# Stick-breaking attention weights written in place over their logarithms, on one Trainium2 core

## The chip, the cores and the metric

The kernel is one program on one core of a Trainium2 chip. It computes two small models one after the other from inputs in the chip's memory. The metric is the device time of one execution in microseconds (us). The engines are TensorE (PE in the rows; PEld its weight loads), VectorE (DVE), ScalarE (ACT), GpSimd (POOL) and SyncE (SP), which issues the loads of the weights.

## The reference

The first block (two layers: differential attention and mLSTM, then a gated spatial mixer) comes first and is not touched. The second block begins with a hybrid mixer over 16 meta tokens and 512 tokens of width 1024. Cut to what matters, its attention is:

```python
def stick_breaking_attention(q, k, v):          # (B, L, 16 heads, 64)
    for q0, q1 in bounds:                       # the 16 meta tokens, then blocks of 128 queries
        z = einsum("bqhd,bkhd->bhqk", q[:, q0:q1], k[:, :q1]) * scale
        log_beta = log_sigmoid(z)
        log_fail = where(causal, log_beta - z, 0.0)
        survive = cumsum(log_fail, axis=3, reverse=True) - log_fail
        a = where(causal, exp(log_beta + survive), 0.0)
        o = einsum("bhqk,bkhd->bqhd", a, v[:, :q1])
```

Beside it run a short causal convolution with gates, two projections with sigmoid gates, an output projection, and after the mixer a gated MLP.

## The kernel before

Every matmul is in float32 and is made of three passes over a weight that is rounded into a high part and a rest: ScalarE writes `w_hi` from `raw` (`split`, L652), VectorE writes `w_lo` (its `split`, L2119), and TensorE multiplies hi by hi, hi by lo and lo by hi. SyncE loads a weight tile of 128 x 1024 into one of four slots of `raw`. ScalarE and VectorE make a tile ready three tiles ahead (`AHEAD`) of its use.

The input projection of the second block goes in eight pairs of heads (`p` = 0 to 7). A pair takes eight weight tiles (`t` = 0 to 7): q, k, v, b, c, h and the two gates. A tile is made in two halves of the tokens (`halves`, L1799 to L1801), each of 24 matmuls into its own bank of `pj`, and the next tile writes the same two banks. So each bank must be emptied within the time of one half. `take` on ScalarE copies q (L1056), k (L1058), v, b (L1068) and c (L1070) out of it, VectorE's L2776 (`conv_in`) multiplies c with the sixth tile, h, for the convolution and so empties tile 5's banks, and ScalarE's tanh (L1073) empties those of tiles 6 and 7.

The attention of pair p-1 is threaded through pair p. It has four query blocks, d = 0 to 3, with (d+1) x 128 keys and the 16 meta keys, for two heads at once. After the even tile t = 2d TensorE does `pair_scores` (scores of block d into `zz`, counted in the semaphore `z`) and then `turn_pair` of block d-1, counted in `turned`; after tile 0 those are block 0 and block 3 of the pair before that. A `turn_pair` transposes the weights of 16 meta keys from `s_am`, and 2(d+1) squares of 128 x 128 from `s_a` into `tr`. At the head of the odd tile t = 2d+1 ScalarE does `logs` of block d: Abs of `zz` into `s_e` (L1035, or L1037 and L1038 for d = 3), Exp (L1039) and Ln (L1040) in place; behind that on its queue stand a `split` and the copies of that tile. VectorE waits for the logarithms and does `weights` (L2679): maximum and sum (L2691), two scans (L2697), and a difference (L2702), all in `s_e`; in tile 5 the second `conv_in` stands between the scans and the difference. In the next even tile ScalarE's own `weights` takes the exponential of `s_e` into `s_am` (L1046) and `s_a` (L1047), counted in `a`. VectorE's `copy_turned` (L2709, L2710) waits for `turned` and copies the transposed weights out of `tr` and `aux`, and `pair_values` multiplies them with v.

The attention of pair 7 is threaded in the same way through the eight tiles of the projection of the convolution (`branch`), after `c_hi` and `c_lo` have been made of the convolution's output; there VectorE's gate products L2721 empty `pj`. After it, `items` (L1992 to L1996) multiply the attention's output `a_hi`, and wait for all the gate products.

The order of each engine's work is written out by hand; an engine does its instructions in order and waits on counting semaphores.

Of the kernel before, what the change touches and what calls it, by code (L numbers as in the profile page):

```python
# [17 lines left out]
ACT = mybir.ActivationFunctionType  # L18
# [5 lines left out]
P = 128  # L24
# [15 lines left out]
def need(eng, sem, n):  # L40

    if not (isinstance(n, int) and n <= 0):
        eng.wait_ge(sem, n)
# [23 lines left out]
def two_models(  # L67
# [6 lines left out]
    _, T, D = x.shape  # L74
    KD = D // P
    NT = T // P
    NM = meta_tokens_2.shape[0]
# [53 lines left out]
    with ExitStack() as ctx:  # L131
# [3 lines left out]
        def sems(stage, names):  # L135
            return {n: sem(f"{stage}_{n}") for n in names.split()}
# [9 lines left out]
        def sb(reg, name, shape, dt=F32):  # L146
            n = 2 if dt == BF16 else 4
            for s in shape[1:]:
                n *= s
            t = nc.alloc_sbuf_tensor_at(name, shape, dt, offset=reg[1])  # L150
            reg[1] += (n + 31) // 32 * 32
            assert reg[1] <= reg[2] + 31, (name, reg)
            return t

        def again(reg, skip=0):
            return [reg[0], reg[0] + skip, reg[2]]

        const = region(4960 + 4 * P + 64 + 4 * NM)
        ident = sb(const, "ident", [P, P])
# [105 lines left out]
        w_ = again(W)  # L265
# [15 lines left out]
        w_ = again(W)  # L281
# [21 lines left out]
        w_ = again(W, 218272 - 187488)  # L303
# [17 lines left out]
        w_ = again(W)  # L321
# [26 lines left out]
        w_ = again(W)  # L348
# [10 lines left out]
        w_ = again(W, AT_W)  # L359
# [1 line left out]
        cc, cv = turns(("cc", [P, TA]), ("cv", [P, TA]))  # L361
        cx = sb(w_, "cx", [P, TA + KW2 - 1])
        s_e = sb(w_, "s_e", [P, 2, TF])
        s_a = sb(w_, "s_a", [P, 2, T])
        s_zm = sb(w_, "s_zm", [P, 2, NM])
        s_am = sb(w_, "s_am", [P, 2, NM])
        s_aT = sb(w_, "s_aT", [P, 2, NT, P])
# [5 lines left out]
        w_ = again(W)  # L373
# [14 lines left out]
        def bank(name, n=1):  # L388
            return ctx.enter_context(nc.psum_tensor(name, [P, n, 512], F32))
# [3 lines left out]
        tr = bank("tr", 2)  # L393
# [28 lines left out]
        MX = sems("mix", "half q k v b c x g conv vturned vtok z log w a turned probsT pv o ychi yclo pc "  # L422
                         "meta_step ahi alo pa mhi mlo")
# [220 lines left out]
        def _(act):  # L644
# [61 lines left out]
            for name, src in ROWS[0]:  # L706
                a = col[name][1]
# [137 lines left out]
            for c in range(NT):  # L845
                ins = act.activation(m_kd0[:, 1, c, :], zz[:, 0, c * P:(c + 1) * P], ACT.Exp, bias=acol[:, c, 0:1])
# [180 lines left out]
            def logs(pr, d, table=True):  # L1027

                n, j = (d + 1) * P, pr * NT + d
                if table and d in (0, NT - 1):  # L1030
                    act.preload_act_table_set("natural_log_exp_and_others")
                act.wait_ge(MX["z"], j + 1)
                need(act, MX["a"], j)
                if d < NT - 1:
                    link(act.activation(s_e[:, :, 0:NM + n], zz[:, :, 0:NM + n], ACT.Abs))  # L1035
                else:
                    act.activation(s_e[:, :, NM:NM + n], zz[:, :, 0:n], ACT.Abs)  # L1037
                    link(act.activation(s_e[:, :, 0:NM], s_zm[:], ACT.Abs))  # L1038
                link(act.activation(s_e[:, :, 0:NM + n], s_e[:, :, 0:NM + n], ACT.Exp, scale=-1.0))  # L1039
                act.activation(s_e[:, :, 0:NM + n], s_e[:, :, 0:NM + n], ACT.Ln, bias=1.0).then_inc(MX["log"], 1)  # L1040

            def weights(pr, d):
                n, j = (d + 1) * P, pr * NT + d
                act.wait_ge(MX["w"], j + 1)
                need(act, MX["turned"], j)
                act.activation(s_am[:], s_e[:, :, 0:NM], ACT.Exp)  # L1046
                act.activation(s_a[:, :, 0:n], s_e[:, :, NM:NM + n], ACT.Exp).then_inc(MX["a"], 1)  # L1047

            def take(t, p, par, hf, first, src=None):

# [45 lines left out]
            def pair(p, par, prev=True, prev2=True, first=False):  # L1096

                for t in range(8):
                    if first and t < NSLOT:
                        if t == 0:  # L1100
                            first_four()
                        continue
                    if t % 2 and prev:
                        logs(p - 1, t // 2)
                    split(P_0 + t + AHEAD, p, 8)
                    if t < 5:
                        act.wait_ge(MX["half"], p * 8 + (t + 1))
                        take(t, p, par, 0, not prev2)
                    if t == 0 and prev2:
                        weights(p - 2, NT - 1)  # L1110
                    if t and t % 2 == 0 and prev:
                        weights(p - 1, t // 2 - 1)
                    if t > 5:
                        act.wait_ge(MX["half"], p * 8 + (t + 1))
                        take(t, p, par, 0, not prev2)
                    if t != 5:
                        finished(P_0 + t, p, 8)
                        take(t, p, par, 1, not prev2)
# [32 lines left out]
            branch(0)  # L1151
            meta_logs()
            weights(p - 1, NT - 1)
            branch(1)
            act.wait_ge(MX["meta_step"], META_STEP["weights"])
            act.activation(s_me[:], s_me[:], ACT.Exp).then_inc(MX["meta_step"], 1)
            logs(p, 0, table=False)
            branch(2)
            weights(p, 0)
            logs(p, 1)  # L1160
            branch(3)
            branch(4)
# [104 lines left out]
        def _(pe):  # L1267
# [131 lines left out]
            for r, n in enumerate(nrows):  # L1399
                ins = pe.transpose(tt[:, 0, r * P:r * P + n], vrow[0:n, r, :], ident[0:n, 0:n])  # L1400
            ins.then_inc(S["turned"], 1)
            pe.wait_ge(S["meta_in"], 32)
            for k in range(KD):
                ins = pe.transpose(rb[:, 0, (KD + k) * NM:(KD + k + 1) * NM], mt[:, k * P:(k + 1) * P],
                                   ident[0:NM, 0:NM])
            pe.wait_ge(S["meta_step"], SETUP_META["scaled"])
            for k in range(KD):
                ins = pe.transpose(rb[:, 0, k * NM:(k + 1) * NM], xmeta[:, k * P:(k + 1) * P], ident[0:NM, 0:NM])
# [174 lines left out]
            for c in range(NT):  # L1583
                ins = pe.matmul(zz[:, 0, c * P:(c + 1) * P], ident_b[:], mask_ge[:], start=False, stop=(c == NT - 1),
                                skip_group_check=True)
# [6 lines left out]
            for c in range(NT):  # L1592
                ch = slice(c * P, (c + 1) * P)
                ins = pe.matmul(zz[:, 1, ch], m_kT[:, ch], m_qT[:, ch], start=True, stop=True)
            ins.then_inc(ML["products"], 1)
            pe.wait_ge(DA["y"], HD - 1)
            for t in range(NT):
                ins = pe.transpose(rb[:, 0, t * P:(t + 1) * P], m_kT[:, t * P:(t + 1) * P], ident[:])
# [143 lines left out]
            for g in range(SG):  # L1742
                ins = pe.transpose(zz[:, g // NT, (g % NT) * P:(g % NT + 1) * P], wsp[:, g, :], ident[:])
            ins.then_inc(SV["turned"], 1)
            for b, dst in enumerate((oo, aux)):
                ins = pe.matmul(dst[:, 0, :], ones[0:1, :], brow[:, b * NT:(b + 1) * NT, :], start=True, stop=True)
# [79 lines left out]
            def turn_pair(pr, d):  # L1826
                j = pr * NT + d
                pe.wait_ge(MX["a"], j + 1)
                need(pe, MX["probsT"], j)
                pe.transpose(aux[0:2 * NM, 0, 512 - P:512], s_am[:].rearrange("p c n -> p (c n)"), ident[:])  # L1830
                for c in range(2):
                    for k in range(d + 1):
                        ins = pe.transpose(tr[:, c, k * P:(k + 1) * P], s_a[:, c, k * P:(k + 1) * P], ident[:])  # L1833
                ins.then_inc(MX["turned"], 1)

            def pair_values(pr, d, par):
# [1232 lines left out]
```

## Time and profile before

| | us |
|---|---|
| median of 3 runs | 1941.81 |
| lowest and highest | 1941.48, 1943.69 |
| the profiled execution, its own time | 1941.62 |
| its span in the trace | 1939.9 |
| TensorE busy | 1924.9 |
| VectorE, ScalarE, GpSimd busy | 1030.8, 764.8, 67.0 |
| mean granted clock of TensorE | 0.999 of full |

The span is the time between the first and the last instruction that the profiler records. A matmul's record is longer than the step from one matmul to the next, since they are pipelined: in the second block's projection a matmul starts every 0.12 us and is recorded with 0.28. So TensorE's busy time says only that it hardly ever stood idle. In the timeline a row gives the start, the duration, and in brackets the idle time before it on its engine and what ended that. `x2` at a row's end merges two instructions. The second block's projection lies between about 985 and 1388 us of the span, the projection of the convolution between 1389 and 1452.

### The profile page before, as it was taken

Reading aid. Unit: us, or ns where it says so; the run is one execution under the profiler, and the core shown is the slowest. Engines: PE = TensorE matmul, PEld = TensorE weight load, DVE = VectorE, ACT = ScalarE, POOL = GpSimd, SP = SyncE. Lnnn points to the kernel's source line nnn. Section 1 sums busy time; section 2 is a strip of 40 time slices with the busy share of each in tenths; the row PEclk is TensorE's granted clock in tenths of the full one; section 3 lists DMA queues with packets and bytes.
Section 4 is the critical chain, followed back from the end, with each engine's and each line's share of the span. In section 5 each row is a group of like instructions: output and inputs, shape, how many; then the busy total and the mean of one; then the engine's idle time right before and its main releaser. Section 6 shows DMA issues by size and latency. Waiting matters only on the chain.

```text
span 1939.9 us, 31396 instructions
## 1 busy us (share of the span) xinstructions
PE 1924.9 (99%) x12104; PEld 1695.6 (87%) x12104; DVE 1030.8 (53%) x1601; ACT 764.8 (39%) x1268; POOL 67.0 (3%) x118
## 2 busy tenths in 40 slices
PE   8999999999999999999999999999999999999998
PEld 8888888889888788888999999999999798999886
DVE  5777767544253555532645655555766364444333
ACT  5544443333233333322435555555642243323222
POOL 3000000000020000000100000000000010000000
PEclk9999999999999999999999999999999999999999
DMA  6222212232323333323232222222222232333321
GB/s 175 80 68 74 76 55 77 78 85 87 119 77 98 99 88 89 91 89 120 79 96 77 67 76 77 74 80 66 69 74 88 77 109 87 91 94 96 104 92 55
DMA packets 244004, 167.27 MB, mean 86 GB/s; under 512 B 5294, under 2 KB 231702, under 8 KB 243911
## 3 DMA queue, kind: packets, MB, share of 16 engines
q1 hardware_dynamic: 242224, 160.98, 27.9%
q10 hardware_dynamic: 1286, 4.23, 0.7%
q8 instruction: 70, 1.15, 0.2%
q0 software_dynamic: 400, 0.72, 0.1%
q14 instruction: 24, 0.19, 0.0%
HBM read 163.81 MB, written 2.10 MB: 86 GB/s over the span
## 4 chain that ended last, share of the span: by engine, by line
PE 97%; DVE 2%; DMA 1%; ACT 0%; issue 0%; SPq 0%; POOL 0%; ACTq 0%; DVEq 0%
PE pj L1799 9%; PE pj L1801 9%; PE pj L1800 9%; PE pj L1279 8%; PE pj L1280 8%; PE pj L1281 8%; PE zz L1280 2%; PE zz L1279 2%; PE zz L1281 2%; PE zz L1336 2%; PE tr L1336 2%; PE zz L1338 2%; PE tr L1338 2%; PE tr L1337 2%; PE zz L1337 2%; PE pj L1336 2%
## 5 line engine op out<-in xcount | busy, mean ns | idle before, releaser
L2119 DVE TENSOR_TENSOR w_lo<-raw,w_hi 128x1024 fp32r<-128x1024 f32 x299 | 365.1, 1223 | 276.6 <-ACT w_hi L652 273.6
L652 ACT ACTIVATE w_hi<-raw 128x1024 fp32r<-128x1024 f32 x299 | 314.5, 1055 | 214.7 <-PE tr L1338 141.2
L1799 PE MATMUL pj<-x_hi,w_hi 128*128 128x258 f32 (+1 forms) x1280 | 365.0, 285 | 0.0
L1801 PE MATMUL pj<-x_hi,w_lo 128*128 128x258 f32 (+1 forms) x1280 | 361.6, 283 | 0.0
L1800 PE MATMUL pj<-x_lo,w_hi 128*128 128x258 f32 (+1 forms) x1280 | 361.0, 282 | 0.0
L1279 PE MATMUL pj<-x_hi,w_hi 128*128 128x512 f32 x632 | 254.0, 402 | 0.0
L1280 PE MATMUL pj<-x_lo,w_hi 128*128 128x512 f32 x632 | 249.8, 395 | 0.0
L1281 PE MATMUL pj<-x_hi,w_lo 128*128 128x512 f32 x632 | 248.4, 393 | 0.0
L1800 PEld LDWEIGHTS pj<-x_lo,w_hi 128*128 128x128 f32 x1280 | 241.7, 189 | 0.8
L1799 PEld LDWEIGHTS pj<-x_hi,w_hi 128*128 128x128 f32 x1280 | 241.3, 189 | 0.9
L1801 PEld LDWEIGHTS pj<-x_hi,w_lo 128*128 128x128 f32 x1280 | 241.3, 189 | 0.0
L1281 PEld LDWEIGHTS pj<-x_hi,w_lo 128*128 128x128 f32 x632 | 118.9, 188 | 27.0
L1279 PEld LDWEIGHTS pj<-x_hi,w_hi 128*128 128x128 f32 x632 | 118.8, 188 | 26.7 <-issue 0.8
L1280 PEld LDWEIGHTS pj<-x_lo,w_hi 128*128 128x128 f32 x632 | 118.8, 188 | 25.2
L1542 PE MATMUL pj<-w_hi,x_hi 128*128 128x256 f32 x256 | 72.8, 285 | 0.0
L1543 PE MATMUL pj<-w_hi,x_lo 128*128 128x256 f32 x256 | 71.9, 281 | 0.0
L1544 PE MATMUL pj<-w_lo,x_hi 128*128 128x256 f32 x256 | 71.9, 281 | 0.0
L2709 DVE COPY s_aTm<-oa 32x128 f32<-32x128 f32 x32 | 8.9, 278 | 110.2 <-PE tr L1833 110.1
L1280 PE MATMUL zz<-x_lo,w_hi 128*128 128x512 f32 x160 | 63.5, 397 | 0.0
L1279 PE MATMUL zz<-x_hi,w_hi 128*128 128x512 f32 x160 | 63.0, 394 | 0.0
L1281 PE MATMUL zz<-x_hi,w_lo 128*128 128x512 f32 x160 | 62.9, 393 | 0.0
L586 POOL TENSOR_SCALAR n_ms<-n_ms 128x1 f32<-128x1 f32 x32 | 14.2, 445 | 1339.0 <-ACT scaled L671 1302.8
(601 smaller groups left out, 3712.3 us busy)
## 6 DMA issues: line engine op xcount, KB each, us to landing
raw<-in_l_w_in_dram SPq DMA_DIRECT2D x113, 512.0 KB, 4.1
raw<-in_w_in_dram SPq DMA_DIRECT2D x64, 512.0 KB, 4.0
raw<-in_w_up_gate_dram SPq DMA_DIRECT2D x44, 512.0 KB, 3.8
raw<-in_l_w_out_dram SPq DMA_DIRECT2D x32, 512.0 KB, 3.4
raw<-in_w_down_dram SPq DMA_DIRECT2D x22, 512.0 KB, 3.4
raw<-in_w_proj_conv_dram SPq DMA_DIRECT2D x8, 512.0 KB, 4.0
raw<-in_w_proj_attn_dram SPq DMA_DIRECT2D x8, 512.0 KB, 4.1
raw<-in_w_out_dram SPq DMA_DIRECT2D x8, 512.0 KB, 3.5
```

The lines of the kernel that those rows point to most:

```text
L652: act.activation(w_hi[:, slot], raw[:, slot], ACT.Copy).then_inc(hi_done, 1)
L1279: pe.matmul(dst, w_hi[:, slot, k, :], hi(k), start=(first and k == 0), stop=False)
L1280: pe.matmul(dst, w_hi[:, slot, k, :], lo(k), start=False, stop=False)
L1281: ins = pe.matmul(dst, w_lo[:, slot, k, :], hi(k), start=False, stop=(last and k == KD - 1))
L1336: pe.matmul(dst[:, nh, :], hi[:, k, tok], w_hi[:, slot, w, :], start=start, stop=False)
L1337: pe.matmul(dst[:, nh, :], lo[:, k, tok], w_hi[:, slot, w, :], start=False, stop=False)
L1338: ins = pe.matmul(dst[:, nh, :], hi[:, k, tok], w_lo[:, slot, w, :], start=False, stop=stop)
L1542: pe.matmul(dst, x_hi[:, k, tok], wh, start=(k == 0), stop=False)
L1799: pe.matmul(dst, w_hi[:, slot, k, :], hi[:, k, tok], start=(k == 0), stop=False)
L1800: pe.matmul(dst, w_hi[:, slot, k, :], lo[:, k, tok], start=False, stop=False)
L1801: ins = pe.matmul(dst, w_lo[:, slot, k, :], hi[:, k, tok], start=False, stop=(k == KD - 1))
L2119: dve.tensor_tensor(w_lo[:, slot], raw[:, slot], w_hi[:, slot].bitcast(F32), ALU.subtract).then_inc(lo_done, 1)
```

## The change

The weights are no longer written into a buffer of their own. ScalarE's `weights` writes the exponential over the logarithms in `s_e`, past the 16 meta columns, and `turn_pair` transposes from there. `s_a` is gone, and the buffers behind it move up in memory. Since `logs` of the next block overwrites `s_e`, it now waits until the turns of the block before are done (`turned`) in place of the exponentials (`a`). `weights` no longer waits for `turned`, which the wait in `logs` covers.

```diff
@@ buffers
-        s_a = sb(w_, "s_a", [P, 2, T])
@@ ScalarE, logs
                 act.wait_ge(MX["z"], j + 1)
-                need(act, MX["a"], j)
+                need(act, MX["turned"], j)
@@ ScalarE, weights
                 act.wait_ge(MX["w"], j + 1)
-                need(act, MX["turned"], j)
                 act.activation(s_am[:], s_e[:, :, 0:NM], ACT.Exp)
-                act.activation(s_a[:, :, 0:n], s_e[:, :, NM:NM + n], ACT.Exp).then_inc(MX["a"], 1)
+                act.activation(s_e[:, :, NM:NM + n], s_e[:, :, NM:NM + n], ACT.Exp).then_inc(MX["a"], 1)
@@ TensorE, turn_pair
-                        ins = pe.transpose(tr[:, c, k * P:(k + 1) * P], s_a[:, c, k * P:(k + 1) * P], ident[:])
+                        ins = pe.transpose(tr[:, c, k * P:(k + 1) * P], s_e[:, c, NM + k * P:NM + (k + 1) * P], ident[:])
```

The waits as they stand in the instructions: ScalarE's queue in tiles 5 and 6 of a pair in the loop over pairs, before. The semaphores of this stage have `mix_` before their names.

```order
L1032 REGISTER_ALU
L1035 ACTIVATE s_e<-zz 128x2x400 [waits mix_a,mix_z]
L55 REGISTER_ALU
L1039 ACTIVATE s_e<-s_e 128x2x400 [waits act_chain]
L55 REGISTER_ALU
L1040 ACTIVATE s_e<-s_e 128x2x400 [waits act_chain]
L652 ACTIVATE w_hi<-raw 128x1024 [waits tile_done,raw_in0]
L651 REGISTER_ALU [waits raw_in1]
L652 ACTIVATE w_hi<-raw 128x1024 [waits tile_done]
L1046 ACTIVATE s_am<-s_e 128x32 [waits mix_turned,mix_w]
L1047 ACTIVATE s_a<-s_e 128x2x384
L1114 REGISTER_ALU
```

And the same stretch with the change:

```order
L1031 REGISTER_ALU
L1034 ACTIVATE s_e<-zz 128x2x400 [waits mix_turned,mix_z]
L55 REGISTER_ALU
L1038 ACTIVATE s_e<-s_e 128x2x400 [waits act_chain]
L55 REGISTER_ALU
L1039 ACTIVATE s_e<-s_e 128x2x400 [waits act_chain]
L651 ACTIVATE w_hi<-raw 128x1024 [waits tile_done,raw_in0]
L650 REGISTER_ALU [waits raw_in1]
L651 ACTIVATE w_hi<-raw 128x1024 [waits tile_done]
L1044 ACTIVATE s_am<-s_e 128x32 [waits mix_w]
L1045 ACTIVATE s_e<-s_e 128x2x384
L1112 REGISTER_ALU
```

The instructions and their order stay; the Abs at the head waits for `turned` where it waited for `a`, the Exp of the meta columns waits for the difference alone, and the Exp of the keys, the row below it, writes `s_e`.

ScalarE's queue in tile 7, before (`REGISTER_ALU` and `ISA` rows are the queue's own waits and counters):

```order
L1037 ACTIVATE s_e<-zz 128x2x512 [waits mix_a,mix_z]
L1038 ACTIVATE s_e<-s_zm 128x2x16
L55 REGISTER_ALU
L1039 ACTIVATE s_e<-s_e 128x1056 [waits act_chain]
L55 REGISTER_ALU
L1040 ACTIVATE s_e<-s_e 128x1056 [waits act_chain]
L652 ACTIVATE w_hi<-raw 128x1024 [waits tile_done,raw_in2]
L1114 REGISTER_ALU
L1073 ISA [waits mix_half]
L1073 ACT_TABLE_LOAD
L1073 ACTIVATE gates<-pj,hbg 128x258
L656 REGISTER_ALU
```

With the change:

```order
L1036 ACTIVATE s_e<-zz 128x2x512 [waits mix_turned,mix_z]
L1037 ACTIVATE s_e<-s_zm 128x2x16
L55 REGISTER_ALU
L1038 ACTIVATE s_e<-s_e 128x1056 [waits act_chain]
L55 REGISTER_ALU
L1039 ACTIVATE s_e<-s_e 128x1056 [waits act_chain]
L651 ACTIVATE w_hi<-raw 128x1024 [waits tile_done,raw_in2]
L1112 REGISTER_ALU
L1071 ISA [waits mix_half]
L1071 ACT_TABLE_LOAD
L1071 ACTIVATE gates<-pj,hbg 128x258
L655 REGISTER_ALU
```

Between the Abs with its new wait and the tanh of `gates` the queue is as it was.

## Rows read from the trace of the kernel before

**Rows 1.** The page's part 1, and the list of waits (us in total, times, longest).

```profile
PE 1924.9 (99%) x12104; PEld 1695.6 (87%) x12104; DVE 1030.8 (53%) x1601; ACT 764.8 (39%) x1268; POOL 67.0 (3%) x118
PE pj L1799 <- DVE gates L2721: 0.5, 1, 0.5
```

**Rows 2.** Timeline, tile 5 of two pairs: start us, us, engine, line, operation [idle before <-releaser].

```profile
1196.01 0.84 ACT L1035 ACTIVATE s_e<-zz 128x800 f32<-128x800 f32 x1 [1.42 <-PE zz L1822]
1196.55 0.28 DVE L2709 COPY s_aTm<-oa 32x128 f32<-32x128 f32 x1 [5.51 <-PE tr L1833]
...
1199.64 1.23 DVE L2119 TENSOR_TENSOR w_lo<-raw,w_hi 128x1024 fp32r<-128x1024 f32 x1 [2.21 <-ACT w_hi L652]
...
1204.31 0.43 DVE L2776 TENSOR_TENSOR cx<-cc,pj 128x258 f32<-128x258 f32 x1 [0.21 <-DVE s_e L2697]
1204.97 0.28 PE L1799 MATMUL pj<-x_hi,w_hi 128*128 128x258 f32 x1
...
1375.35 0.42 DVE L2776 TENSOR_TENSOR cx<-cc,pj 128x258 f32<-128x258 f32 x1
...
1376.17 0.28 PE L1799 MATMUL pj<-x_hi,w_hi 128*128 128x258 f32 x1
```

**Rows 3.** Timeline, ScalarE, TensorE and VectorE around tile 7 of the same pair.

```profile
1208.81 1.28 ACT L1031 ACT_TABLE_LOAD   x1
...
1210.12 1.03 ACT L1037 ACTIVATE s_e<-zz 128x1024 f32<-128x1024 f32 x1
...
1210.89 0.28 DVE L2709 COPY s_aTm<-oa 32x128 f32<-32x128 f32 x1 [1.08 <-PE tr L1833]
...
1215.77 0.48 ACT L1073 ACTIVATE gates<-pj,hbg 128x258 f32 x1
...
1216.42 0.34 PE L1799 MATMUL pj<-x_hi,w_hi 128*128 128x258 f32 x1
...
1216.72 0.48 ACT L1073 ACTIVATE gates<-pj,hbg 128x258 f32 x1 [0.47 <-PE pj L1801]
```

**Rows 4.** Timeline, the heads of tiles 1 and 3 of the next pair.

```profile
1224.10 0.41 ACT L1035 ACTIVATE s_e<-zz 128x288 f32<-128x288 f32 x1
...
1225.07 0.28 DVE L2709 COPY s_aTm<-oa 32x128 f32<-32x128 f32 x1 [3.18 <-PE tr L1833]
...
1228.00 0.39 ACT L1058 ACTIVATE s_k<-pj 128x264 f32<-128x264 f32 x1 [1.58 <-PE pj L1801]
...
1238.89 0.63 ACT L1035 ACTIVATE s_e<-zz 128x544 f32<-128x544 f32 x1 [1.73 <-PE zz L1822]
...
1239.21 0.28 DVE L2709 COPY s_aTm<-oa 32x128 f32<-32x128 f32 x1 [5.54 <-PE tr L1833]
```

**Rows 5.** Timeline, TensorE waits for a gate product in the conv projection.

```profile
1396.32 0.76 DVE L2721 SCALAR_TENSOR_TENSOR gates<-gates,pj 128x258 f32<-128x258 f32 x2
...
1396.89 0.35 PE L1799 MATMUL pj<-c_hi,w_hi 128*128 128x258 f32 x1 [0.55 <-DVE gates L2721]
1397.09 0.28 PE L1800 MATMUL pj<-c_lo,w_hi 128*128 128x258 f32 x1
```

**Rows 6.** Timeline, the last pair's attention in the conv projection.

```profile
1439.30 0.41 DVE L2721 SCALAR_TENSOR_TENSOR gates<-gates,pj 128x258 f32<-128x258 f32 x1
...
1440.30 0.28 PE L1799 MATMUL pj<-c_hi,w_hi 128*128 128x258 f32 x1
...
1444.66 1.03 ACT L1037 ACTIVATE s_e<-zz 128x1024 f32<-128x1024 f32 x1 [3.75 <-PE zz L1822]
...
1451.85 0.42 DVE L2721 SCALAR_TENSOR_TENSOR gates<-gates,pj 128x258 f32<-128x258 f32 x1
...
1452.33 0.39 PE L1992 MATMUL pj<-a_hi,w_hi 128*128 128x258 f32 x1
```

**Rows 7.** Busy time by stretch: PE, PEld, DVE, ACT, POOL (count); granted clock, DMA share, GB/s.

```profile
1395.00:1400.00 5.00, 4.46 (x50) 4.23 (x48) 4.93 (x23) 2.86 (x6) 0.00 (x0) 1.00 0.00 0
...
1421.00:1426.00 5.00, 5.00 (x31) 4.72 (x30) 1.12 (x1) 2.21 (x4) 0.00 (x0) 0.66 0.37 105
```

## The prediction

> **What bounds the kernel now.** I read the page first. TensorE is busy for 1924.9 us, 99% of the span, and in the list of waits it stood, in the whole execution, waiting for VectorE on the second block's `pj` for 0.5 us in all, once [rows 1]. So nothing the change does to ScalarE's or VectorE's busy time matters; what matters is whether it makes TensorE wait. For that I read the timeline of one pair tile by tile. A pair is eight weight tiles (0 to 7), each of two halves of 24 matmuls, 2.87 us a half at 0.12 us a matmul. After an even tile TensorE does the attention work: the scores of block d into `zz`, then the turns of block d-1. ScalarE meets the new scores at the head of the next odd tile, and behind `logs` on its queue stand the rounding of a weight tile and the copies that empty `pj`.
>
> **What the change does to that queue.** Arithmetic and counts stay: 32 exponentials write `s_e` where they wrote `s_a`, and 160 transposes read it. In place costs nothing that a row shows: L1039 and L1040 already work from `s_e` to `s_e`. One wait moves. `weights` no longer waits for `turned`; that wait was long satisfied (the turns of block d-1 end a whole tile earlier), so it gives nothing. `logs` waits for `turned` instead of `a`. TensorE issues the turns right behind the scores, so ScalarE's Abs, which now starts 0.04 us after the last score matmul, will start after the last transpose. VectorE's copy L2709 waits for just that semaphore today, so its start is my measure of the release. The Abs moves by the difference of the two rows: for d=2, 1196.55 - 1196.01 = 0.54 us [rows 2]; for d=3, 1210.89 - 1210.12 = 0.77 us [rows 3]; for d=0 of the next pair, 1225.07 - 1224.10 = 0.97 us, and for d=1, 1239.21 - 1238.89 = 0.32 us [rows 4]. Everything queued behind the Abs on ScalarE moves along, unless it had idle time before it.
>
> **Tile 1 and tile 3 (d=0, d=1): nothing.** In tile 1 the first copy behind, `s_k`, had 1.58 us of idle before it [rows 4]; 0.97 fits. In tile 3 everything may slip by the 0.32; the copy `cb` behind it empties a half bank that TensorE wants again only after one more half, 2.87 us. VectorE's w_lo slips too, but a tile is rounded three tiles (some 17 us) ahead of its use. If that cover were gone, each pair would cost up to 1.3 us more.
>
> **Tile 5 (d=2): seven times.** Abs, Exp, Ln and then the rounding end 0.54 later, and VectorE's w_lo sits idle waiting for exactly that rounding (2.21 us idle, released by w_hi) [rows 2]. Behind it on VectorE, back to back, stand the first conv product, the block's maximum and scans, and the second conv product, L2776, which frees the second half of `pj` for tile 6. It ends at 1204.74 and TensorE starts that half at 1204.97 [rows 2]: 0.23 us. What a release costs I take from the one existing stall of this kind: VectorE's first gate product starts at 1396.32 and, at 0.42 us (the row of one such product in [rows 6]), ends at 1396.74; TensorE starts at 1396.89, so 0.15, and the matmul behind comes after 0.20 instead of 0.12 us, another 0.08 for a restart [rows 5]. Slack is therefore 0.23 - 0.15 = 0.08, and the stall 0.54 - 0.08 + 0.08 = 0.54 us. Four pairs look like this. In the first and the last two, which stand outside VectorE's loop, L2776 ends 0.40 before its reader (1375.77 against 1376.17) [rows 2]: 0.54 - 0.25 + 0.08 = 0.37 us. Sum: 4 x 0.54 + 3 x 0.37 = **3.3 us**. Bounds: 0 (if a release takes no longer and VectorE picks the delay up in its idle 2.21) and 7 x 0.62 = 4.3.
>
> **Tile 7 (d=3): seven times, the last one mild.** Abs, Abs of `s_zm`, Exp, Ln, rounding, a table load of 1.28 us and the gate's tanh run on ScalarE without a gap from 1210.12 to 1216.25, 6.13 us. The tanh empties the first half of `pj`, and TensorE starts the next pair's tile 0 there at 1216.42, 0.17 us later [rows 3]. That is what a release costs (0.15 above), and the distance is the same 0.17 at all six places where a pair follows a pair: TensorE starts on the release, and the slack is zero. The 0.77 us passes in full, with 0.08 for the restart: 0.85 x 6 = 5.1. (A stall in tile 6 shifts scores, turns and ScalarE alike, so the two do not cover each other.) After the seventh pair comes the first tile of the conv projection, whose bank waits through c_hi and c_lo. These stand behind the second gate, which has 0.47 us of idle before it in every pair [rows 3], so that 0.77 - 0.47 = 0.3 is left at most; the second gate also starts a little before the first has ended, and I take 0.2. Together **5.3 us**; bounds 0 and 7 x 0.85 = 6.0.
>
> **The last pair's attention, inside the projection.** The weight tiles here have more attention work between them. For d=2 the gate product behind the logarithms ends at 1439.71, 0.59 us before its reader at 1440.30 [rows 6]: 0.54 - 0.59 + 0.15 = 0.1, with the restart 0.2; d=0 and 1 have more room. Tight is d=3: Abs 1444.66 and the same 0.77 to the end of the turns, through rounding, w_lo and the block's maximum to the gate product that ends at 1452.27; TensorE starts the output of `a_hi` at 1452.33, waiting for it [rows 6]: 0.8. Together **1.0 us**, bounds 0 and 1.1. VectorE's scan and weights shift with it, TensorE too, so the last turn costs nothing more.
>
> **Sum.** 3.3 + 5.3 + 1.0 = 9.6 us. The profiled execution took 1941.6 us (1.7 around its span), 0.2 under the median shown, so 1951.2 and, against the median, 1951.4; I say 1951.3.
>
> **A rule against this change.** The rows show ScalarE 0.77 us ahead of the turns, which the second buffer allows it, and TensorE with hardly a gap [rows 1, 3]. The Trainium skill, in "Perfetto Trace Analysis", section "Optimization Strategy", says that a gap that repeats on the engine that should be saturated can mean too few buffers in SBUF. By that rule every one of the 31 hand-overs of the one buffer left would show as a gap, and the sum would be the second rival's 19.8 us in place of 9.6.
>
> **Rivals.**
> *Only the hard deadline costs.* Tile 5's delay vanishes in VectorE's idle time or in a shorter release. For: 2.21 us of idle stand there. Against: that idle is waiting for the very rounding that is late. 1941.8 + 5.3 + 0.8 = 1947.9. 7%.
> *Every block pays.* If no idle time and no bank time covers anything, each Abs's lateness comes out at the end: 8 x (0.32 + 0.54 + 0.77) + 7 x 0.97 = 19.8 us: 1961.6. Against: 1.58 us idle in tile 1. 3%.
> *The clock.* After the small matmuls of the meta queries the granted clock averages 0.66 in 1421 to 1426, and is 1.00 (2.4 GHz) in 1395 to 1400 [rows 7]: for part of these 5 us it was at 1.2 GHz, and 0.34 x 5 = 1.7 us were lost. All else stays as forecast, but this work now comes 8.5 us later. If the drop does not come: 1949.6, 30%. If the new stalls bring more of them (each 1.7, two to four), 1954.5 to 1958, 5%; against that, the existing stall of 0.55 us lies in a clock of 1.00 [rows 5, 7]. The Trainium skill, "TensorE: Matmul & The Clock Gate", Part 1, has the clock follow how busy the engine has lately been; no run here yet shows whether 0.85 us pauses count.
> *Not slower.* One mechanism: ScalarE is released not by the last transpose but reaches the Abs later anyway. In tile 7 a table load ends at 1210.09 [rows 3]; if it came 0.8 us later, the turns would be done and the new wait would be free, in tile 7 and by the same lateness in tile 5, where there is no table load. Then nothing is left of 9.6, and the clock's 1.7 may come back: 1940 to 1942. It decides from 1210.89, the release; ScalarE is 0.77 us ahead of it in every pair. That the change does not do what it says belongs here, if the release of `turned` had come first all along; the rows show Abs ahead of L2709 each time. 3%.
>
> **How the numbers follow.** Forecast with its exact mechanism 52%, and 30% for the same with the clock back; 7, 3, 5 and 3% for the rest. A measurement of this kernel tells about 0.2% (3.9 us) from no change, so slower means over 1945.7: all but the last rival and a little of the first, 0.95; same 0.04, faster 0.01. The range leaves out the outer rivals: low 1948.4 (the clock back and no restart cost, 1949.6 less 15 x 0.08), high 1953.2 (all stalls at their upper bounds, 11.4).
>
> **What would show it.** In the new profile: Abs of d=2 and d=3 start with L2709, and their idle is laid to the transposes. TensorE's waits gain a row on the gates' tanh (six, about 0.8 each) and one on L2776 (seven, 0.3 to 0.5). Tiles 1 and 3 keep their pace. TensorE's busy time stays near 1925 us while the span grows by 9 to 10. ScalarE's `weights` starts no earlier against TensorE. I am wrong if the stalls are there but the span is not longer by their sum, or if tile 0 starts within 0.1 us of its old distance from tile 7.

## The result, and the profile after

| | before | with the change |
|---|---|---|
| median, us | 1941.77 (5 runs) | 1952.71 (5 runs) |
| all, us | 1941.48, 1941.75, 1941.77, 1941.81, 1943.69 | 1950.94, 1951.25, 1952.71, 1952.90, 1952.91 |
| ratio, 95% interval | | 1.0049, 1.0037 to 1.0060 |
| the profiled execution | 1941.62 | 1952.91 |

The kernel before ran again beside each group of experiments, and their ratios are against these runs: median 1941.96 us (26 runs) for `wait_only`, `two_buffers`, `own_d3` and `own_d2`, 1943.14 (16 runs) for `own_d2_w3`, `turns_first` and the two with a doubled Abs, 1942.91 (22 runs) for `scores_first`, `turns_first_sa` and `spread_meta`; one of these last 22 was a slow execution of 4422.14 us, which the ratios leave out.

The changed kernel is slower by 0.5%. The page of its profile, parts 1 and 4, against [rows 1] and against part 4 of the page before (second fence): TensorE's busy time grew by 5 us and the span by 11.3, and the chain of work that ended last now passes through ScalarE and VectorE for 3% each, where it was 0% and 2%.

```profile
span 1951.2 us, 31365 instructions
PE 1930.1 (99%) x12104; PEld 1697.5 (87%) x12104; DVE 1030.5 (53%) x1601; ACT 762.3 (39%) x1268; POOL 66.8 (3%) x118
PE 92%; DVE 3%; ACT 3%; issue 2%; DMA 1%; SPq 0%; ACTq 0%; POOL 0%; DVEq 0%
```

```profile
PE 97%; DVE 2%; DMA 1%; ACT 0%; issue 0%; SPq 0%; POOL 0%; ACTq 0%; DVEq 0%
```

TensorE's list of waits (us in total, times, longest) has three rows that were not there, six waits for the gates' tanh, four for the second conv product, and one for the last gate product. The wait for `c_lo`, at the head of the conv projection, was there before with 0.4 us (second fence, from the trace before) and has grown to 0.6:

```profile
PE pj L1797 <- ACT gates L1071: 3.7, 6, 0.6
PE pj L1797 <- DVE cx L2774: 1.1, 4, 0.3
PE pj L1990 <- DVE gates L2719: 0.9, 1, 0.9
PE pj L1310 <- DVE c_lo L2806: 0.6, 1, 0.6
```

```profile
PE pj L1312 <- DVE c_lo L2808: 0.4, 1, 0.4
```

These waits are shorter than the stalls, since a matmul is recorded with 0.28 us and the next is due 0.12 us after its start: idle appears only past the recorded end. So I read a stall from the distance between the starts. In the timeline of the changed kernel, tile 5 of the pair that [rows 2] show:

```profile
1200.77 0.28 DVE L2707 COPY s_aTm<-oa 32x128 f32<-32x128 f32 x1 [5.23 <-PE tr L1831]
1200.83 0.84 ACT L1034 ACTIVATE s_e<-zz 128x800 f32<-128x800 f32 x1 [2.03 <-PE tr L1831]
...
1204.46 1.23 DVE L2117 TENSOR_TENSOR w_lo<-raw,w_hi 128x1024 fp32r<-128x1024 f32 x1 [2.81 <-ACT w_hi L651]
...
1209.13 0.42 DVE L2774 TENSOR_TENSOR cx<-cc,pj 128x258 f32<-128x258 f32 x1 [0.21 <-DVE s_e L2695]
...
1209.61 0.39 PE L1797 MATMUL pj<-x_hi,w_hi 128*128 128x258 f32 x1 [0.27 <-DVE cx L2774]
```

The Abs starts 0.06 us behind the copy that waits for the turns, and its idle time is laid to the transposes. VectorE's idle before w_lo grew from 2.21 to 2.81 us, and TensorE stands waiting for the conv product. Tile 7 and the head of the next pair, against [rows 3, 4]:

```profile
1215.70 1.03 ACT L1036 ACTIVATE s_e<-zz 128x1024 f32<-128x1024 f32 x1 [0.79 <-PE tr L1831]
...
1221.34 0.84 ACT L1071 ACTIVATE gates<-pj,hbg 128x258 f32 x2
1221.96 0.36 PE L1797 MATMUL pj<-x_hi,w_hi 128*128 128x258 f32 x1 [0.63 <-ACT gates L1071]
...
1230.71 0.41 ACT L1034 ACTIVATE s_e<-zz 128x288 f32<-128x288 f32 x1 [1.05 <-PE tr L1831]
...
1233.58 0.39 ACT L1056 ACTIVATE s_k<-pj 128x264 f32<-128x264 f32 x1 [0.56 <-PE pj L1799]
```

The tanh of the first half starts at 1221.34, ends 0.48 later (its duration in [rows 3]) at 1221.82, and TensorE starts at 1221.96. In tile 1 the idle before `s_k` shrank from 1.58 to 0.56 us, and TensorE noticed nothing.

Of the growth of 11.3 us, 9.6 are there when TensorE starts L1990, at 1461.97 where it was 1452.33 [rows 6]. Not all of that is the change: TensorE is 0.36 us later already behind the first scores, before any block meets the new wait (the second matmul behind them starts at 998.35 where it was 997.99), and 0.28 of that is there after the first 10 us of the program. In the traces of the other versions that place lies between 0.15 us early and 0.42 late, once the clock is allowed for, so this is spread between executions, and 9.3 us belong to the change. The other 1.7 come at a place that the change does not touch. Busy time by stretch (PE, PEld, DVE, ACT, POOL; granted clock, DMA share, GB/s) and the timeline there:

```profile
1425.00:1435.00 10.00, 10.00 (x72) 9.29 (x71) 5.92 (x10) 3.90 (x7) 0.00 (x0) 0.83 0.38 105
1555.00:1560.00 5.00, 5.00 (x24) 4.26 (x24) 1.48 (x4) 0.11 (x1) 0.00 (x0) 0.66 0.00 0
```

```profile
1553.89 1.91 PE L2041 MATMUL oa<-sel,hl_t 8*128 8x4 f32 x16 [0.24 <-DVE hl_t L2914]
1555.73 0.67 PE L1334 MATMUL pj<-w_hi,m_hi 128*128 128x512 f32 x1
```

The half-clock stretch of [rows 7] is still there (1425 to 1435 is that work, later), and there is a second one behind 16 small matmuls of 4 columns. The kernel before has the same 16 small matmuls, and in its profiled execution no fall comes behind them:

```profile
1544.19 1.92 PE L2043 MATMUL oa<-sel,hl_t 8*128 8x4 f32 x16 [0.24 <-DVE hl_t L2916]
1546.04 0.50 PE L1336 MATMUL pj<-w_hi,m_hi 128*128 128x512 f32 x1
```

Such a stretch costs 1.7 us and comes or stays away from one execution to the next. That fits the times of each kernel, which stand in groups some 1.3 to 2.0 us apart. The mean granted clock goes with them: in the changed kernel it is 0.999 for the two executions of the lower group and 0.998 for the three of the upper. In what follows I compare profiled executions after taking off 1.7 us for each half-clock stretch: without any, before comes to 1939.9 and the changed kernel to 1949.5, a difference of 9.6. With the spread of 0.4 us at the start, a difference of this kind is good to about half a microsecond.

### The profile page after: what moved, and what is told of

It reads as the page before. It is cut to its first block, busy times and chain, and to the rows that moved or that the text cites. A ratio compares the mean times of both kernels' runs of the same rounds, so it can differ in the third digit from the quotient of the medians.

```text
span 1951.2 us, 31365 instructions
## 1 busy us (share of the span) xinstructions
PE 1930.1 (99%) x12104; PEld 1697.5 (87%) x12104; DVE 1030.5 (53%) x1601; ACT 762.3 (39%) x1268; POOL 66.8 (3%) x118
## 4 chain that ended last, share of the span: by engine, by line
PE 92%; DVE 3%; ACT 3%; issue 2%; DMA 1%; SPq 0%; ACTq 0%; POOL 0%; DVEq 0%
PE pj L1797 8%; PE pj L1799 8%; PE pj L1798 8%; PE pj L1277 8%; PE pj L1278 8%; PE pj L1279 7%; PE zz L1278 2%; PE zz L1277 2%; PE zz L1279 2%; PE zz L1334 2%; PE pj L1334 2%; PE tr L1334 2%; PE zz L1336 2%; PE tr L1336 2%; PE pj L1336 2%; PE tr L1335 2%
```

## The experiments

**1. Is it the wait or the in-place write?** The kernel before with the waits alone:

```diff
-                need(act, MX["a"], j)
+                need(act, MX["turned"], j)
...
                 act.wait_ge(MX["w"], j + 1)
-                need(act, MX["turned"], j)
```

> The kernel before with the waits of the change and nothing else: the weights still go to s_a. My theory (the wait alone costs, by making the logarithms start after the turns): the same time as the changed kernel, before + 9.6 us, some 1951.4, or 1.7 more in executions in which the clock drops once more; TensorE's stalls before tile 0 (six, 0.92 us gap between matmuls) and before tile 6's second half (four of 0.56, three of 0.39) are all there. Rival (writing and turning in place costs, by the buffer or the moved addresses): most of the 9.6 goes away, 1942 to 1945.

Measured: 1951.06 us median (1950.77 to 1952.50), ratio 1.0049 (1.0035 to 1.0063). The profiled execution has one half-clock stretch, 1951.06, so 1949.4 without. Its waits are those of the changed kernel to the tenth:

```profile
PE pj L1798 <- ACT gates L1072: 3.7, 6, 0.6
PE pj L1798 <- DVE cx L2775: 1.1, 4, 0.3
```

The whole loss is the wait, within 0.1 us. Writing in place, and reading the transposes from there, costs nothing that shows.

**2. In place with two buffers.** The changed kernel with `s_e0` (400 columns) for blocks 0 and 2 and `s_e1` for 1 and 3 (the cut leaves out that `weights` waits for `turned` again, since `s_am` is still one buffer, and that each user picks its buffer from the list; the same holds for experiments 3 and 4):

```diff
-        s_e = sb(w_, "s_e", [P, 2, TF])
+        s_e0 = sb(w_, "s_e0", [P, 2, 400])
+        s_e1 = sb(w_, "s_e1", [P, 2, 528])
+        s_es = [s_e0, s_e1, s_e0, s_e1]
...
-                need(act, MX["turned"], j)
+                need(act, MX["turned"], j - 1)
```

> The changed kernel, in place, but with two buffers s_e, one for blocks 0 and 2 (cut to the 400 columns that they need) and one for blocks 1 and 3; the logarithms wait for the turns of two blocks before. My theory: all stalls gone, within 0.5 us of the kernel before, 1941.8. Rival (in place costs): stays at 1950 or more. Rival (the clock): small differences of 1.7 us from it in some executions.

Measured: 1942.94 us median (1941.53 to 1945.01, 11 runs), ratio 1.0004 (0.9995 to 1.0013). The profiled execution took 1941.53 with one stretch, none of the new waits, and the clock fell at the other place (1545 to 1550) and not at the first:

```profile
1415.00:1435.00 20.00, 20.00 (x168) 18.98 (x166) 12.77 (x22) 9.20 (x15) 0.00 (x0) 1.00 0.20 57
1545.00:1550.00 5.00, 5.00 (x22) 4.25 (x21) 1.23 (x4) 1.09 (x2) 0.00 (x0) 0.66 0.00 0
```

**3. A buffer of its own for block 3.** `s_es = [s_e0, s_e0, s_e0, s_e1]`, and the wait in `logs`:

```diff
-                need(act, MX["turned"], j)
+                need(act, MX["turned"], (j - 1, j, j, j - 3)[d])
```

> The changed kernel with a buffer of its own for block 3 alone, so the wait is free for block 3 (tile 7) and stays for block 1 and 2. My theory: tile 7's 5.3 and the 0.8 at the end go, tile 5's 3.3 and 0.2 stay: before + 3.5, 1945.3. Rival (only the hard deadline of tile 7 costs, and the rest comes from the clock or elsewhere): 1941.8 to 1943. Rival (each block pays its lateness, 19.8 us cut down by something): tile 3's 8 x 0.32 would stay as well, + 6.

Measured: 1946.81 us median (1945.45 to 1948.91, 10 runs), ratio 1.0024 (1.0014 to 1.0033). The profiled one took 1946.67 with two stretches, 1943.3 without: 3.4 above before, for 3.5 expected. The wait of block 0 is relaxed here too, for the block before it in the buffer is now block 2; tile 1 had room in any case. TensorE's waits keep the conv product and lose the gates' tanh:

```profile
PE pj L1800 <- DVE cx L2777: 1.1, 4, 0.3
```

**4. A buffer of its own for block 2.** `s_es = [s_e0, s_e0, s_e1, s_e0]`, with the waits `(j, j, j - 3, j - 1)[d]`.

> The changed kernel with a buffer of its own for block 2 alone, so the wait is free in tile 5 and stays in tiles 1, 3 and 7. My theory: tile 5's 3.5 goes and 6.1 stay: 1947.9, with TensorE's six gaps of 0.92 us before tile 0 and none above 0.13 before tile 6's second half. The savings of this and of the own buffer for block 3 add up to the whole loss, since a stall shifts scores, turns and ScalarE alike. Rival (the two stalls cover each other): each alone saves less than its part, the two savings sum to under 8.

Measured: 1943.41 us median (1940.29 to 1945.25, 11 runs), ratio 1.0004 (0.9995 to 1.0013), so 4.5 us less than I expected. The fault lay in the experiment. With block 2 elsewhere, block 3 overwrites what block 1 left, whose turns are done before tile 5 begins, so its wait in tile 7 had come free as well. Two blocks of four still share a buffer with their forerunner here (0 and 1), and nothing is lost: a small confirmation that tiles 1 and 3 have room. (For block 0 the forerunner is block 3 of the pair before.) The second try keeps block 3's wait, `(j, j, j - 3, j)[d]`.

> The kernel with a buffer of its own for block 2, once more, now with the wait of the change kept for block 3: in the run before, block 3's last user of the buffer was block 1, so its wait had come free as well and nothing of tile 7's cost was left in it. My theory: tile 5's stalls are gone, tile 7's six (0.92 us gap before tile 0) and the last pair's stay: before + 6.1, so 1947.9 with as many clock drops as the kernel before has in most executions, 1949.6 with one more. Rival (tile 7's deadline bites only when tile 5 has been late): under 1945.

Measured: 1948.41 us median (1947.95 to 1949.85, 6 runs), ratio 1.0030 (1.0018 to 1.0043). The profiled one took 1949.79 with two stretches, 1946.4 without: 6.5 above before, for 6.1 expected. One wait of the six was longer here (0.9 against some 0.6 for the rest), and that is most of the excess.

```profile
PE pj L1800 <- ACT gates L1074: 4.1, 6, 0.9
```

Its two stretches, with the columns as above:

```profile
660.00:670.00 10.00, 10.00 (x34) 7.08 (x33) 5.66 (x9) 1.84 (x3) 1.03 (x1) 0.83 0.57 168
1550.00:1560.00 10.00, 9.76 (x49) 8.19 (x48) 3.78 (x9) 1.97 (x5) 2.07 (x4) 0.83 0.01 2
```

Here a third place had the half clock, in the first block, behind four matmuls whose operands have a single row (`brow` and `ones`, 1.98 us for the four). 3.4 and 6.5 make 9.9, where the whole is 9.6 (with the start of each execution taken into account 3.6 and 6.4, and 9.3): the two stalls do not cover each other.

**5. The lateness without the wait.** The kernel before, with both buffers and its own waits, and the Abs of block 3 done twice:

```diff
+                    link(act.activation(s_e[:, :, NM:NM + n], zz[:, :, 0:n], ACT.Abs))
                     act.activation(s_e[:, :, NM:NM + n], zz[:, :, 0:n], ACT.Abs)
...
```

(The other changed line gives ScalarE's loop its new count of chained instructions.)

> The kernel before with the Abs of block 3 done twice, one after the other (1.03 us more on ScalarE at the head of tile 7, no wait added and no buffer taken away). My theory (zero slack from ScalarE's Abs in tile 7 to the next pair's tile 0): TensorE's gap before tile 0 grows from 0.17 to about 1.2 six times, 6 x 1.13 = 6.8, 0.5 behind the seventh pair, 1.1 at the end: before + 8.4, 1950.2. Rival (it is the wait for another engine, and not its lateness, that costs): before + 0 to 2.

Measured: 1951.15 us median (1950.91 to 1952.71, 5 runs), ratio 1.0046 (1.0032 to 1.0060). The profiled one took 1951.24 with two stretches, 1947.8 without: 7.9 above before, for 8.4. So it is ScalarE's lateness that costs, with the new wait or without it:

```profile
PE pj L1800 <- ACT gates L1074: 5.3, 6, 0.9
```

The same for blocks 0 and 1:

```diff
+                if d < 2:
+                    link(act.activation(s_e[:, :, 0:NM + n], zz[:, :, 0:NM + n], ACT.Abs))
...
```

> The kernel before with the Abs of blocks 0 and 1 done twice (0.41 and 0.63 us more at the head of tiles 1 and 3, sixteen times). My theory (tiles 1 and 3 have room): within 0.5 us of the kernel before. Rival (every block pays its lateness): 8 x (0.45 + 0.66) = 8.9 more, 1950.7.

Measured: 1943.14 us median (1941.48 to 1943.65, 11 runs), ratio 1.0002 (0.9993 to 1.0011), and no new wait of TensorE; the profiled one took 1941.48 with one stretch. Sixteen delays of 0.4 to 0.6 us vanish in tiles 1 and 3.

**6. Can one buffer be had for nothing?** TensorE's attention work in another order, in the changed kernel and in the kernel before (abridged, each word stands for the lines of that step):

```diff
                     if t % 2 == 0:
-                        (values) (scores) (turns)
+                        (turns) (scores) (values)
```

> The changed kernel, one buffer, with TensorE's attention work in another order in the pairs: turns, then scores, then the values, where it was values, scores, turns. Scores then end with the turns already done, and as the values (0.68 to 0.90 us) are longer than the turns (0.46 to 0.74), no later than in the kernel before. My theory: all stalls in the pairs gone, the 1.0 us of the last pair stays (its order is not changed): 1942.8. Rival (a single buffer costs by itself, in whatever order): 1950 or more. Rival (the new order only moves the wait, to TensorE's turns waiting for the weights): a new row of PE tr waiting for ScalarE's exponentials, some 1945.

> The kernel before (both buffers, its own waits) with the order turns, scores, values in the pairs. In the changed kernel this order took away all stalls, and yet each of the 32 gaps between two tiles was 0.23 us longer, so 7.4 us. My theory: the order alone costs this on TensorE (the load of 64-row scores behind 128-row transposes), so before + 7.4: 1949.3 with one clock drop, 1951 with two. Rival (the 0.23 comes from reading the transposes from s_e, or from ScalarE at work in the same buffer): within 1 us of before.

Measured with one buffer: 1950.73 us median (1949.10 to 1950.96, 5 runs), ratio 1.0040 (1.0026 to 1.0054); the profiled one 1950.73 with two stretches, 1947.3 without, 7.4 above before where 1.0 was expected. With both buffers: 1949.17 us median (1947.87 to 1950.02, 6 runs), ratio 1.0034 (1.0022 to 1.0046); the profiled one 1948.59 with one stretch, 1946.9 without, 7.0 above before where 7.4 were expected (0.4 of the 7.0 are there before the first pair's attention, so 6.6). My theory for the first run was wrong, and its stalls were gone all the same: TensorE's waits have neither the tanh nor the conv product. The time went into TensorE's own work. The gap after tile 6, before (first fence) and with turns first in one buffer (second):

```profile
1207.72 0.28 PE L1801 MATMUL pj<-x_hi,w_lo 128*128 128x258 f32 x1
1207.84 0.38 PE L1843 MATMUL oa<-s_aTm,s_vmp 128*128 128x128 f32 x2
1208.15 0.66 PE L1847 MATMUL oa<-s_aT,s_vt 128*64 128x128 f32 x8
1208.74 1.13 PE L1815 MATMUL zz<-s_k,s_q 64*128 64x512 f32 x4
1209.80 0.28 PE L1822 MATMUL zz<-mask_lt,ident_b 128*128 128x128 bf16 x2
1209.92 0.27 PE L1830 MATMUL oa<-ident,s_am 128*32 128x128 f32 x1
1210.03 0.82 PE L1833 MATMUL tr<-ident,s_a 128*128 128x128 f32 x6
1210.61 0.37 PE L1799 MATMUL pj<-x_hi,w_hi 128*128 128x258 f32 x1
```

```profile
1210.94 0.28 PE L1799 MATMUL pj<-x_hi,w_lo 128*128 128x258 f32 x1
1211.07 0.27 PE L1828 MATMUL oa<-ident,s_am 128*32 128x128 f32 x1
1211.17 0.82 PE L1831 MATMUL tr<-ident,s_e 128*128 128x128 f32 x6
1211.92 1.13 PE L1813 MATMUL zz<-s_k,s_q 64*128 64x512 f32 x4
1212.98 0.29 PE L1820 MATMUL zz<-mask_lt,ident_b 128*128 128x128 bf16 x2
1213.11 0.44 PE L1841 MATMUL oa<-s_aTm,s_vmp 128*128 128x128 f32 x2
1213.47 0.66 PE L1845 MATMUL oa<-s_aT,s_vt 128*64 128x128 f32 x8
1214.06 0.39 PE L1797 MATMUL pj<-x_hi,w_hi 128*128 128x258 f32 x1
```

From the last projection matmul to the first of the next tile it is 2.89 us before and 3.12 with the other order, for the same instructions. Six transposes take 0.58 us to the start of what follows when that is the projection, and 0.75 when it is the scores, whose weights have 64 rows; the first values take 0.36 instead of 0.31. Not 32 gaps grew, as I had put into the expectation of the second run, but 27, 26 of them by 0.23 and one by 0.06: 6.05 in all. With the 1.0 of the last pair that makes 7.1 of the 7.4 of the first run; and the matmul behind each of the 26 gaps comes 0.02 to 0.03 later than before, while the six waits of 0.05 before tile 0 are gone. That 32 x 0.23 also gives 7.4 was chance: the 1.0 of the last pair was in the time that I had divided. The second run shows that it is the order and not the buffer, since it has the same gaps with `s_a` kept. Why scores behind transposes cost more is not shown: eight values take 0.59 us to what follows them whether that is the scores or the projection.

**7. The scores first.** The kernel before in the order scores, values, turns.

> The kernel before (both buffers, its own waits) with TensorE's attention work in the pairs in the order scores, values, turns. ScalarE meets the scores 0.7 to 0.9 us earlier. My theory: the six waits of 0.05 us before tile 0 go, and the first tile of a pair is paced by TensorE alone: 0.3 us less than before, 1941.5 in executions with one clock drop, which no median can tell apart; the trace's gap before tile 0 goes from 0.17 to 0.12. Rival (what stands beside what on TensorE counts for more, as in the order with turns first, where each of the 32 gaps was 0.23 us longer): before + 1 to 7 us.

Measured: 1946.83 us median (1943.86 to 1948.82, 11 runs), ratio 1.0016 (1.0007 to 1.0025); the profiled one 1945.38 with one stretch, 3.8 above before. The rival held: the gap after tile 6 is 3.05 us, 0.16 longer, and 26 gaps of this kind, 4.2 us, outweigh the 0.3 us won. The order of the kernel before is the shortest of the three.

**8. The clock.** The kernel before, with the eight small value products of the meta queries (16 matmuls in the trace, two for each) laid one by one between the eight steps of a projection tile:

```diff
-            meta_queries(3)
             pair_values(p, 0, 1)
-            branch(4)
...
+            branch(4, between=meta_value)
```

> The kernel before with the eight small value products of the meta queries (4 columns each, 1418.8 to 1420.8 us) laid one by one between the eight steps of the next projection tile, same work. My theory of the clock (a stretch of small matmuls lets the granted clock fall to 1.2 GHz for a few us, 1.7 us lost, at one of three places from execution to execution): the granted clock stays 1.00 from 1415 to 1435 and executions of some 1940.2 and 1941.9 appear in place of 1941.8 and 1943.4. Rival (the drop comes at a fixed time, or from the attention work): the half-clock stretch stays, and the time with it.

Measured: 1946.54 us median (1942.03 to 1947.00, 11 runs), ratio 1.0015 (1.0006 to 1.0024); the profiled one 1945.48 with two stretches, near 665 and 1550 us, and none in the place of the edit (first fence, the kernel before in the second):

```profile
1415.00:1435.00 20.00, 20.00 (x150) 18.03 (x150) 11.09 (x21) 8.92 (x14) 0.00 (x0) 1.00 0.19 54
```

```profile
1415.00:1435.00 20.00, 20.00 (x155) 19.10 (x154) 11.08 (x18) 9.36 (x14) 0.00 (x0) 0.91 0.19 54
```

The clock of 1.00 there proves nothing for the edit: the profiled executions of `wait_only`, `two_buffers`, `own_d2_w3` and `turns_first_sa` show it at this place too, without the edit. The price can be read: TensorE did 150 matmuls in these 20 us, where before it was 155 at a mean clock of 0.91. In its timeline three large matmuls and two small ones take 0.87 us from one step of the projection to the next:

```profile
1424.63 0.39 PE L1799 MATMUL pj<-c_hi,w_hi 128*128 128x258 f32 x1
...
1425.50 0.39 PE L1799 MATMUL pj<-c_hi,w_hi 128*128 128x258 f32 x1
```

Apart from each other the three take 0.36 and two of the sixteen 0.24 (1.87 us from the first of the 16 to what follows them, before), so each of the eight places costs 0.27, 2.2 in all. Without stretches the execution comes to 1942.1, which is 2.2 above before. So both theories fell as to the time: executions of 1940.2 did not appear (the fastest is 1942.03). Whether spreading keeps the clock up stays open, and the other times speak against it: six of the 11 stand at 1946.5 to 1947.0, some 4.7 above the fastest, with a mean granted clock of 0.997 where the profiled one with its two stretches has 0.998. That is what three falls would give, and only three places are known, one of them that of the edit. No trace of such an execution was kept.

No version tried is faster than the kernel before. The in-place write with two buffers is its equal and needs 400 + 528 = 928 columns for each of the two heads, where `s_e` and `s_a` needed 528 + 512 = 1040.

## Why the prediction was right

*The release.* Right as to what releases the Abs, and a little short as to when. The Abs starts 0.06 us behind the copy that waits for the turns, where I had taken the same time for both. Against the last score matmul it moved by 0.38, 0.60, 0.83 and 1.04 us for d = 1, 2, 3 and 0, each 0.06 more than I read from the copy (0.07 for d = 0).

*Tiles 1 and 3 cost nothing.* Right: the new profile has no wait of TensorE there, and 16 added delays cost nothing.

*Tile 5, 3.3 us.* Right. The distance between matmuls before tile 6's second half is 0.56 us in four pairs and 0.39 in three; less 0.12, and with 0.10 for the restart (the next matmul comes after 0.22), 0.54 and 0.37, as in the sum. That it fits to the hundredth is partly luck, since two of its terms were off and cancel: the Abs came 0.06 later than taken, and the release of TensorE by the conv product takes 0.06 us (the product ends at 1209.55, TensorE starts at 1209.61, and so in all seven), not the 0.15 that I took from a gate product. The slack was therefore 0.17 and not 0.08. The row of one of the three, which follows its forerunner by 0.39 and shows no idle of its own since that is under the recorded length:

```profile
1326.28 0.39 PE L1797 MATMUL pj<-x_hi,w_hi 128*128 128x258 f32 x1
```

*Tile 7, 5.3 us.* Right. The distance is 0.89 to 0.92 where it was 0.17, and 0.07 for the restart: 0.8, for 0.85 in the sum. Behind the seventh pair the wait for c_lo grew from 0.38 to 0.61 us, 0.2 as taken; my reading of the list of waits, one wait of 0.5 us on this `pj`, had left out those 0.38. Together that is 5.1 us for 5.3. TensorE starts that matmul 8.68 us later than before, 8.3 without the 0.36 from before the pairs, where the two terms had 8.6:

```profile
1398.55 0.36 PE L1310 MATMUL pj<-c_hi,w_hi 128*128 128x258 f32 x1 [0.61 <-DVE c_lo L2806]
```

*The last pair, 1.0 us.* Right: from there to L1990 another 0.96.

```profile
1461.97 0.39 PE L1990 MATMUL pj<-a_hi,w_hi 128*128 128x258 f32 x1 [0.94 <-DVE gates L2719]
```

*The sum.* The forecast sum was 9.6 us. The stalls measure 9.3, and the two profiled executions differ by 9.6 only with the 0.36 us from before the pairs: the size is right to 0.3 us, the full agreement is chance.

*The median.* It moved by 10.9 us. I had given the clock one place and asked only whether it would fall there. There are three, the kernel before mostly has one or two falls per execution, and among the five executions of the changed kernel three had two, where of before's five one did, going by the groups of their times. 1951.3 is the lower group (1950.94 and 1951.25), the median lies in the upper. It is inside the range by 0.5 us, but not for a reason that I gave: 1953.2 was reckoned from longer stalls with the clock as it was, and what used up that room was one more fall of the clock, which the range did not provide for. That part of being right is luck.

*The signs.* Two of my signs came out otherwise than written: TensorE's busy time grew by 5.2 us instead of staying near 1925 (1.7 from the second half-clock stretch, and an estimated 3.4 of the 9.3 us of stalls, since the waits in the lists grew by only 5.9), and the rows of waits are six of 0.6 and four of 0.3, not six of 0.8 and seven of 0.3 to 0.5. The reason is the same for both: a stall shows as idle only past the recorded end of the matmul before it, and the three short stalls of tile 5 not at all.

*The rivals.* Of the rivals, *only the hard deadline* fell with experiment 3 (tile 7's stalls gone, 3.4 us left) and with the stalls before tile 6's second half, *every block pays* with the doubled Abs of blocks 0 and 1, and *not slower* with the rows of the Abs. Of *the clock*, the part in which the new stalls bring falls of their own did not happen: the granted clock stays 1.00 through all 13 stalls of 0.4 to 0.8 us, and in all 13 profiled executions of this study, as long as TensorE has work, it falls only at three places, each behind matmuls that have few columns or few rows. The Trainium skill, "TensorE: Matmul & The Clock Gate", Part 1, has the clock follow how busy the engine has been. The trace neither bears that out nor contradicts it: stalls of 0.8 us changed nothing, and just ahead of the falls TensorE stood idle for at most 0.24 us; no run here shows what the falls answer to. The rule of the Trainium skill, "Perfetto Trace Analysis", section "Optimization Strategy", on repeated gaps and missing buffers names the cause of the 13 gaps rightly; that every one of the 31 hand-overs costs did not hold, and would have made twice the loss.

## What to carry to other kernels

Where an engine that is always busy hands over banks to others, look for the places at which it starts on the release itself (here a distance of 0.17 us in each pair, though the list of waits had no row for it): a wait added upstream of such a place on another engine's queue comes out in full unless idle time lies between, and the same wait in tiles 1 and 3, where there is room, is free. A buffer that is used in turn by successive blocks can be given away for nothing only where the reader's end, not the writer's, comes before the next writer is ready, or where that writer has time to spare. To move the reader forward in the busy engine's order is not free either: in the three orders tried here the same steps took 2.89, 3.05 and 3.12 us.

## What the runs showed of the hardware that I had not expected

- What stands beside what on TensorE has a price: six transposes followed by the scores, with 64-row weights, cost 0.17 us more than followed by the projection, with 128-row ones. The same instructions took 2.89, 3.05 and 3.12 us in three orders.
- The granted clock falls to the 1.2 GHz level for a part of some 5 us (0.66 over 5 us, 1.7 us lost) at one or two of three places (near 665, 1425 and 1550 us) in each of the 13 profiles, each behind matmuls of few columns or few rows, with TensorE idle for at most 0.24 us just ahead of the fall. At which of them it falls changes between executions of nearly the same program: the place near 1425 has it in eight profiles and not in five, the one near 1550 in nine, the one near 665 in two. The times stand in groups some 1.3 to 2.0 us apart and fit none to three such falls. That is as large as many effects that one would like to measure in this kernel, and the granted clock in the profile tells them apart. That the small matmuls bring the fall was not shown: they stand before each one, but the one attempt to move them did not settle it.
- Small matmuls laid between large ones are not free: eight pairs of them cost 0.27 us each over what they and the large ones take apart.
- What a release takes depends on the pair of instructions: 0.06 us from VectorE's conv product to TensorE, 0.14 from ScalarE's tanh to TensorE, and 0.10 from TensorE's last transpose to ScalarE's Abs where VectorE's copy starts 0.04 behind the same transpose.
- A recorded matmul is 0.16 us longer than the pace, so stalls up to that length leave no idle in the trace, and longer ones show 0.16 less.
